# A state-space layer's small steps moved between other stages' matmul tiles, and its scan reordered by groups of heads

## The reference, cut to what matters

```python
x = x + 0.5*m[2]*swiglu(modulate(x, g0, m[0], m[1]), ...)     # norm, then FFN
h = h + 0.5*mc[2]*swiglu(modulate(h, g0, mc[0], mc[1]), ...)  # the same weights
y = ssd_mixer(modulate(x, ...), modulate(h, ...), ...)
#   project both; conv of width 5; silu; softplus of the step sizes dt
#   for each direction d: state after the context -> start state of x's scan
#   y_diag = cb * Lmat * xdt ; y_off = C * h_in * exp(a_cum)     # 2 chunks of 128
#   gy = rmsnorm(y * silu(z)) over each of 4 groups of 512; gy @ w_out
x = x + m[5]*y ; FFN ; second layer: FFN, pooling mixer, FFN
return rmsnorm(x, final_g)
```

## Time and profile before

| | us |
|---|---|
| median of three executions | 3169.97 |
| the profiled execution, its own time | 3170.71 |
| its span, first to last instruction | 3168.7 |

### The profile page before, as it was taken

The page is one execution under the profiler, slowest core; times in us unless marked ns, Lnnn a source line. Parts: engine busy times, 40 slices in busy tenths (PEclk is TensorE's granted clock), DMA queues, the critical chain, the costliest instruction groups (busy, mean ns, idle before and its releaser), DMA issues.

```text
span 3168.7 us, 37416 instructions
## 1 busy us (share of the span) xinstructions
PE 2623.8 (83%) x13870; PEld 1991.5 (63%) x13870; DVE 2208.0 (70%) x3940; ACT 1036.7 (33%) x2181; POOL 727.8 (23%) x683
## 2 busy tenths in 40 slices
PE   7999998897699999999877787877877678876656
PEld 5999986685589999999765254522554235532212
DVE  6886866737637878768515956698666976689675
ACT  4443332112223344343322244233342233322212
POOL 0000000003200000000002433344343433334553
PEclk9999998998899999999888898988989989999879
DMA  7767952240048959759547999999999999999998
GB/s 305 260 235 265 360 201 95 95 146 27 1 164 322 374 223 356 266 212 364 192 159 307 421 409 397 420 413 421 419 420 420 412 398 419 415 413 422 422 417 339
DMA packets 136871, 976.54 MB, mean 308 GB/s; under 512 B 15501, under 2 KB 15509, under 8 KB 18848
## 3 DMA queue, kind: packets, MB, share of 16 engines
q0 software_dynamic: 91088, 661.23, 51.3%
q1 hardware_dynamic: 44496, 308.07, 25.6%
q10 hardware_dynamic: 1152, 5.52, 0.5%
HBM read 973.69 MB, written 1.06 MB: 308 GB/s over the span
## 4 chain that ended last, share of the span: by engine, by line
PE 49%; DMA 24%; DVE 15%; issue 5%; ACT 4%; POOL 1%; DVEq 0%; ACTq 0%; POOLq 0%
PE psum L619 48%; DMA rows<-in_peer,eidx 23%; DVE rows L2138 2%; DVE arena L1616 2%; DVE yacc L1458 2%; DVE arena L1455 1%; DVE wlow L1455 1%; PE psum L622 1%; DVE arena L1458 1%; POOL rows L2273 1%; ACT L1065 1%; DVE arena L1461 1%; DMA arena<-in_ada_t 1%; DVE rep L1929 1%; ACT u L1065 1%
## 5 line engine op out<-in xcount | busy, mean ns | idle before, releaser
L619 PE MATMUL psum<-rows,diag 128*128 128x512 f32 x1440 | 786.8, 690 | 366.0 <-ACT diag L1065 355.6
L2138 DVE CUSTOM_DVE_ANT_0 rows<-rows,h2tok 128x1024 f32<-128x1024 f32 x512 | 626.6, 1225 | 339.4 <-DMA rows<-in_peer,eidx 331.8
L2273 POOL DMA_INDIRECT rows<-in_peer,eidx x512 | 611.8, 1195 | 961.9 <-PE psum L619 558.8
L619 PEld LDWEIGHTS psum<-rows,diag 128*128 128x128 f32 x1440 | 292.2, 215 | 791.4 <-ACT diag L1065 500.1
L619 PE MATMUL psum<-u_hi,whigh 128*128 128x256 f32 x1760 | 505.9, 287 | 21.5 <-DVE u_lo L1458 18.1
L619 PE MATMUL psum<-u_lo,whigh 128*128 128x256 f32 x1760 | 502.2, 285 | 0.0
L619 PE MATMUL psum<-u_hi,wlow 128*128 128x256 f32 x1760 | 501.7, 285 | 0.0
L1455 DVE TENSOR_TENSOR wlow<-wring,whigh 128x2048 fp32r<-128x2048 f32 x165 | 377.0, 2288 | 120.4 <-ACT whigh L1065 115.4
L1065 ACT ACTIVATE whigh<-wring 128x2048 fp32r<-128x2048 f32 x165 | 314.1, 1908 | 193.0 <-PE psum L619 133.9
L619 PEld LDWEIGHTS psum<-u_hi,whigh 128*128 128x128 f32 x1760 | 341.3, 194 | 24.9 <-issue 19.3
L619 PEld LDWEIGHTS psum<-u_lo,whigh 128*128 128x128 f32 x1760 | 342.3, 194 | 0.0
(11 more groups left out here) (270 smaller groups left out, 3224.5 us busy)
## 6 DMA issues: line engine op xcount, KB each, us to landing
arena<-in_ada_t POOLq DMA_DIRECT2D x116, 1024.0 KB, 7.1
wring<-in_ffn_w_gate SPq DMA_DIRECT2D x55, 1024.0 KB, 5.7
wring<-in_ffn_w_up SPq DMA_DIRECT2D x55, 1024.0 KB, 6.6
wring<-in_ffn_w_down SPq DMA_DIRECT2D x55, 1024.0 KB, 6.5
wring<-in_w_in SPq DMA_DIRECT2D x32, 1024.0 KB, 8.8
wring<-in_peer_wq SPq DMA_DIRECT2D x32, 1024.0 KB, 9.3
wring<-in_ssd_w_in SPq DMA_DIRECT2D x30, 1024.0 KB, 4.8
wring<-in_w_out SPq DMA_DIRECT2D x16, 1024.0 KB, 9.5
```

What stands on the lines that cost most here:

```text
L619: return nc.tensor.matmul(out, lhsT, rhs, start=start, stop=stop, skip_group_check=shared)
L2138: v.tensor_tensor_reduce(out=rows[:, n % SLOTS, 0:D], in0=rows[:, n % SLOTS, 0:D], in1=h2tok[:, t, :], scale=1.0, scalar=0.0, op0=ALU.mult ...
L2273: pool.indirect_dma_start(out=rows[:, n % SLOTS, :], out_offset=None, in_=A[f"peer{u // 2}"], in_offset=bass.IndirectOffsetOnAxis(ap=eidx[ ...
```

## The change

It consists of these parts:

1. `ffn(0)` works on h and `ffn(1)` on x. Norm 2 (h) is made inside `ffn(1)`: its sums after PE's second tile, the DVE products after `product(1, 3)`, the shift ahead of ACT's loop.
2. Norm 3's sums come after the context's third projection tile, its products go into `hsq`, not `u`. `ssd_dt`, `ssd_sums` and the turns of the context stand between projection tiles, the last two turns after x's second tile.
3. The context's four states follow x's tiles 3 to 6 instead of 0 to 3, with one buffer `xw` instead of two; each `state_end` is followed by the next `state_begin`. x's dt, sums and turns begin at tiles 7 and 9. PSUM banks are given by two lists.
4. The two states of x, the products of B and C and the first two running sums stand between z's 8 tiles.
5. The scan goes by `for jb, for c, for d`. x times dt is made in pieces of a group of 8 heads, 16 pieces of 512 columns, between the batches. Gate, squares, sums, root, reciprocal and products of a group run beside the next group's batches; `ssd_out`'s first two tiles are begun before the last group is ready.
6. The bias table is made in the pooling stage. The final norm is made after the turn: ACT squares x in token order out of PSUM with a running sum, DVE multiplies by the reciprocal and by `final_g` broadcast over partitions.
7. In `SECOND` the first two key tiles come one place earlier and `score` 1 is made in the step of `score` 0.

```diff
 def ffn(n):                                          # PE
     half(0, bank(4))
     half(1, bank(6))
+    if n == 1:
+        norm_sums(2)
...
-norm_sums(2)
 for i in range(11):
+    if i < 4:
+        pe.wait_ge(x_part, 5 + i)
     project("proj_ctx", i, 11, proj_evicted, 0, u, KB, 64 if i == 0 else 256)
-norm_sums(3)
-ssd_dt(0)
-ssd_sums(0)
-ssd_turn(0, 0, 10)
+    if i == 2:
+        norm_sums(3)
+    if i == 5:
+        ssd_dt(0)
+    if i == 7:
+        ssd_sums(0)
+    if i >= 4 and i % 2 == 0:
+        ssd_turn(0, i - 4, i - 2)
...
+    project("proj_lat", i, 21, proj_evicted, 11, hsq, KB, 64 if i == 0 else 256, LAT_BANKS)
+    if i == 1:
+        ssd_turn(0, 8, 10)
+    if 3 <= i < 7:
+        d = (i - 3) // 2
+        ssd_states(i - 3, first_chunk(d) if i % 2 else 1 - first_chunk(d))
...
+for i in range(8):
...
+    project("proj_lat", i, 21, proj_evicted, 24, hsq, KB, 256, Z_BANKS)
+    if i == 0:
+        ssd_turn(1, 8, 10)
+    if i in (2, 4):
+        ssd_states(3 + i // 2, first_chunk(i // 2 - 1))
+    if i in (3, 5):
+        chunk_products((i - 3) // 2)
+    if i == 6:
+        running_sums(0)
+        running_sums(1)
...
-BATCHES = [(c, jb, d) for c in range(NCH) for jb in range(H // 4) for d in range(2)]
+BATCHES = [(c, jb, d) for jb in range(H // 4) for c in range(NCH) for d in range(2)]
...
     outputs(b)
+    if b in (12, 20, 28):
+        group_sums((b - 12) // 8)
...
+w0 = tile()
+out_part(0, w0, 0, 8)
+group_sums(3)
+out_part(0, w0, 8, 12)
+w1 = tile()
+out_part(1, w1, 0, 12)
+out_part(0, w0, 12, XB)
+out_part(1, w1, 12, XB)

     if lat and i < 4:                                # DVE, ssd_conv, after tile i
+        state_end(i)
+        if i < 3:
+            state_begin(i + 1)
...
+if b % 8 >= 2 and b % 8 < 6 and b < 24:              # DVE, scan
+    i = b % 8 - 2
+    weigh_dt(b // 8 + 1, i // 2, i % 2)
 segments(b)
...
+if b in (10, 18, 26):
+    gated((b - 10) // 8)
+if b in (25, 27):
+    group_scale((b - 25) // 2)
+if b in (26, 28):
+    group_norm((b - 26) // 2)
...
+f(xs[:], x_turn(t), ACT.Square, accum_out=ostat[:, t:t + 1])            # ACT, final
+f(ostat[:, t:t + 1], ostat[:, t:t + 1], ACT.Sqrt, scale=1.0 / D, bias=eps[:, 0:1])
+stt(xres[:, t, :], x_turn(t), ostat[:, t:t + 1], fg[:], ALU.mult, ALU.mult)   # DVE
...
-SECOND = [...] + ["wq", "wq", "wq", "wq", "keys", "wq", "wq", "keys", "wq", "wq", "keys", "keys"]
+SECOND = [...] + ["wq", "wq", "wq", "keys", "wq", "wq", "wq", "keys", "wq", "wq", "keys", "keys"]
+SCORED = [(), (), (0, 1), (), (2,), (3,), (4,), (5,), (6,), (7,)]
```

More of the change, by code:

```diff
@@ L807, in _, with chunk_products @@
[L807 to L811, removed]
+                    pe.wait_ge(proj_evicted, 19)
+                if i >= 9:
+                    ssd_turn(1, 2 * i - 18, 2 * i - 16)
+            def chunk_products(c):
+                if c == 0:
+                    pe.wait_ge(xbc_ready, 22)
+                    pe.wait_ge(decay_ready, 4)
+                else:
+                    pe.wait_ge(cbm_ready, 2)
@@ L858, in _, with out_part @@
                 outputs(b)
-            pe.wait_ge(y_evicted, 16)
[L860 to L867, removed]
+                if b in (12, 20, 28):
+                    group_sums((b - 12) // 8)
+            def out_part(i, w, first, last):
+                for k in range(first, last):
+                    if i == 0 and k in (0, 8, 12):
+                        pe.wait_ge(gnorm_ready, 2 if k == 0 else k // 4 + 1)
+                    ins = mm(bank(i, 0, T), w[:, k * P:(k + 1) * P], xbc[:, k, :], k == 0, k == XB - 1)
+                if last == XB:
+                    ins.then_inc(weights_consumed, 1)
+            w0 = tile()
[6 more added lines that the diff above has]
+            out_part(1, w1, 12, XB)
+            pe.wait_ge(y_evicted, 16)
+            for i in range(2, 8):
                 project("ssd_out", i, 8, so_evicted, 0, xbc, 16, 128)
@@ L897, in _ @@
             ffn(4)
[L898 to L908, removed]
+            for j in range(KB // 2):
+                pe.wait_ge(x_part, 25 + j)
+                for t in range(TT):
+                    for k in (2 * j, 2 * j + 1):
+                        ins = transpose(bank(4 + 2 * t + k // 4, (k % 4) * P, P), xT[:, k, t * P:(t + 1) * P])
+                    if j == KB // 2 - 1:
+                        ins.then_inc(x_turn_done, 1)
             def tile2(n):
@@ L1114, in norm @@
                     return
[L1115 to L1118, removed]
+                shifted(n)
             def high(n, t, it=0):
@@ L1744, in sums, with turned @@
                 tt(diff, tot, acum, ALU.subtract).then_inc(diff_ready, 1)
-            def tokens(lat):
-                sums(lat)
-                for i in range(10):
+            def turned(lat, first, count):
+                for i in range(first, first + count):
                     g, c = i // 2, i % 2
@@ L1858, in _ @@
             skip(31)
[L1860 to L1868 removed]
+            gated(3)
+            for g in (2, 3):
+                group_scale(g)
+                group_norm(g)
             for i in range(8):
@@ L2043, in mix @@
                 yield mix_slot(g, 12)
+                if g == 0:
+                    tables()
                 dve.wait_ge(win_evicted, 8 * g + 4)
```

359 lines of the change are left out of this document (217 added, 142 removed).

## The result

The changed kernel took 3122.88 us (median of 4 executions, 3119.34 to 3127.14) against 3169.7 us for the kernel before in the same comparison: a ratio of 0.986, with a 95% interval of 0.984 to 0.987. It is faster, as forecast, but by 47 us instead of 80, and outside the range (3073 to 3112). Its profiled execution has a span of 3120.8 us, 47.9 less than before, and a mean granted clock of 0.931.

What follows compares the result with a forecast made beforehand. PE was taken as idle in places around the state-space layer, with transfers bounding the last 1463.9 us. Gains 46.4 + 24.5 + 8.6 + 3.3 - 2.5 = 80.3; 3170.7 - 80.3 - 0.7 = 3089.7, forecast 3090 us, range 3073 to 3112.

Steps and rivals of the forecast that it cites:

- I take one stall of 6 us: Context's states: PE waits once, 6 us, for DVE's weights of state 2, plus 1.5 for a slower state afterwards.
- What can still stop PE is DVE, in two places: Before the scan: only the context's stretch (no cost) and the context's states (7.5 us) could make PE wait for DVE.
- The lower bound: Before the scan: DVE bounds all four state steps and x's turns begin late, another 13 us, leaving a gain of 33.
- 85 taken: Scan: DVE's work of about 80 us plus ramp, table load and chain waits gives 85 us, up to 95.
- eight norm products at 0.45, 3.4: Scan: the gated norm's eight products add 3.4 us to DVE's work, at 0.45 each.
- So I leave it inside the 85: Scan: POOL stalled beside DVE's pieces, about 17 us, would be busy 63 of 85 us, so no extra time was added.
- 2 + 55.3: After the scan's last outputs: 2 us of waiting, then eight `ssd_out` tiles at 6.91 each, 55.3 us.
- The one at 3111: Rival, chance 0.16: DVE bounds all four state steps (13 us) and the scan takes 93 us; gain 59.
- PE stays fed: Rival, chance 0.16: no stall at softplus, scan at PE's own 78 to 80 us; 13 us less, 3077.
- The rival with a chance of 0.03: Before the scan, z's tiles wait for banks or turns; half of the 46 us gain is lost, 3113 to 3120.

Runs made afterwards that it cites:

- copies first: Changed kernel, but in the projection of x DVE copies a pair of turned tiles before waiting for the next projected tile: 3096.46 us, 0.977 to the kernel before.
- softplus early: Changed kernel, but x's softplus chain on DVE comes after the first conv tile instead of the second: 3113.43 us.
- the ninth kernel: Changed kernel, but POOL's product of each scan batch is made on 64 of its 512 columns, so the output is not the reference's: 3114.75 us.
- The sixth kernel: Changed kernel, but ACT loads Exp's table before the scan and DVE makes two x times dt pieces after batch 2's segments and weights: 3120.8 us.
- the tenth: Changed kernel with the turns' copies ahead of the tile's wait and x's softplus chain one tile earlier, together: 3087.08 us.

## Why the prediction was wrong

**Before the scan: 21.1 of the 33 us.** Forecast was a gain of 46.4 to the first outputs (near 706); they came at 726.90, a gain of 25.3. The experiments take this stretch apart. From the start of the context's projection, in us:

| kernel | start | first outputs | length |
|---|---|---|---|
| changed | 437.88 | 726.90 | 289.0 |
| copies first | 434.99 | 699.12 | 264.1 |
| softplus early | 435.80 | 716.58 | 280.8 |
| both | 438.18 | 693.65 | 255.5 |

So 289.0 = 255.5 of PE's work + 8.6 for state 2 (264.1 - 255.5) + 24.9 for x's turns (289.0 - 264.1). The first term was forecast as 259.7 (263.3 without norm 2's 3.6), 4.2 too high. The second, "I take one stall of 6 us" with 1.5 for the slow state behind it, was 7.5 against 8.2 to 8.6; the stall itself was 6.02. The step that failed is the sentence "What can still stop PE is DVE, in two places". There was a third, and it isn't a matter of how much DVE has to do. The prediction follows DVE step by step through the four states and stops there: it doesn't say which instruction of DVE stands behind which wait at x's turns, and has no term for them. The lower bound mentions turns that begin late, but as a part of 13 us; they alone were 24.9, so even that bound (a gain of 33) was too good.

**The scan: 8.0 us.** 93 us against 85 taken and 95 as the bound; with `ssd_out` the gain was 16.5 (166.8 less 150.3) instead of 24.5. DVE was the bound, as forecast. But the 85 were 80 us of its work and 5 for all else, and measured were 82.7 and 10.3. Of the work, "eight norm products at 0.45, 3.4" took 5.4, and the pieces some 11 instead of 9.8; gates and reciprocals came as forecast. The step that failed here is "So I leave it inside the 85", which priced the contention as POOL's delay alone. It also lengthens DVE's own products, and since DVE sets the pace the scan pays for it: 5.0 us by the ninth kernel. About 1 us of that the kernel before paid already (31 products at 0.720 instead of 0.687), and the forecast had it through its rows. The 5 us for ramp, table loads and waits were too few by half, for DVE waited 6.9 us for PE and 2.4 for ACT. The sixth kernel's 2.3 us can't be added to the 5.0: 2.0 of them are DVE's busy time, with a pair of products that the ninth shortens as well. So at least 2.3 of the 8.0 us stay open.

**What was right.** The projection began at 437.9 (forecast 439) with no gap before it, so norm 2 inside `ffn(1)` cost PE's own 3.6 us and no more, as far as one trace can tell (the start differs by up to 3.4 us between executions). From the last outputs to the end of `ssd_out` it was 57.2 us at clock 1.00, against 57.3 (2 + 55.3), where the earlier trace rows show 14.25 us idle and 58.05 cold. The end of the block gained 9.1 (8.6 forecast), by the chain of waits:

```profile
1516.38 1.12 ACT xs L1133 x2
...
1518.12 1.30 DVE x_tok L1561
...
1524.72 3.54 PE psum L626 x16
```

The earlier trace rows have that last matmul at 1571.14. Ahead of it the gain had been 37.35, at norm 7's reciprocal. The pooling stage lost 1.9 (2.5 forecast). The first selection gained 2.2 in the two traces and 3.4 when part 7 alone was undone (3.3 forecast); `topv` moved from the earlier trace rows to:

```profile
1634.47 0.88 DVE topv L2063 x4
```

The last stretch, 1464.8 us at a DMA share of 1.00, is as long as before, and nothing was given back.

**The rivals.** The one at 3111 had DVE as the bound in the states and 93 us of scan. It had the scan, but the states closed as forecast. "PE stays fed" failed in the changed kernel; its first half, no stall before the scan, holds in the tenth, but no kernel here has a scan of 78 to 80 us (the shortest is 88.0). The rival with a chance of 0.03, that half of the 46 us before the scan is lost to waits for banks or turns, came nearest in the size of that loss (21.1) and in its kind; it looked for the waits at z's tiles, and they were at x's.

As an account: the forecast gain of 80.3 is 32.4 above the 47.9 of the spans, 21.1 of it before the scan and 8.0 in it. Most of the other 3.3 is no effect of the change: from the end of `ssd_out` to norm 6's reciprocal it takes 415.2 us in the changed kernel and 412.5 in the one before, and 411.8 to 415.3 in the other kernels here, whose code is the same in that stretch.

## What to carry to other kernels

Where two engines hand buffers back and forth in a pipeline, write down for each wait which instruction is queued in front of its releaser. An engine that is idle for nearly half its time (92 of 208 us here) can still be late by 6 us a step, if the copy that frees a bank stands behind a wait for the next tile. Move the release ahead of that wait first: here it cost nothing and gave 25 us. When a step's pace is DVE's, count POOL's products with two SBUF inputs against DVE too, not as free work beside it.

## What the runs showed of the hardware

- A DVE product of 128x1024 with both inputs in SBUF took 1.22 us alone and 2.29 beside a POOL product; one of 128x512 took 0.68 and 1.34 to 1.35. POOL's own went from 1.27 to 3.19. Both engines lose, and DVE's operations on PSUM with one column do not (0.341 and 0.344 us).
- Work added to the engine that sets the pace cost 2.5 times its own duration. The 15.6 us were 6.2 of that work, 5.0 by which DVE was busy beyond it (its products were longer), and 4.4 more of idle time: with the clock down to 0.87 in the scan PE's own work took 7.8 us longer, and DVE's waits for PE rose from 6.9 to 11.4. That the 5.0 are the contention is argued from the ninth kernel, not shown apart.
- Each wait of 6 us at x's turns cost about 8: 18.0 us of waits made up 24.9, the rest being slower turns and tiles behind them (1.94 for 1.04, 7.68 to 9.21 for 7.07, at a granted clock of 0.73 to 0.85 instead of 1.00).
